# Step sizes' weight parts in one stationary operand, and the compression's first layer with gathered blocks stationary

## What is computed

```
u = rms_norm(h, norm_w)
z, xbc, dt = split(u @ in_w, ...)          # dt: 512 x 32
dt = softplus(dt + dt_bias)
```

```
blk = to_g(t)[:, :, cidx] + pe             # 2 groups x 31 blocks x 32 x 64
flat = blk.reshape(B, G, Nc, CMP_BLOCK * dh)
return gelu(flat @ w1) @ w2                # w1: 2048 x 128
```

## Time and profile before

| | |
|---|---|
| median of the runs | 1399.4 us |
| span of the profiled execution | 1396.6 us |
| instructions | 17863 |
| mean granted clock of TensorE | 0.996 |
| TensorE busy | 1355.5 us (97%) |
| VectorE busy | 831.2 us (60%) |
| ScalarE busy | 680.4 us (49%) |
| POOL busy | 529.8 us (38%) |

### The profile page before, as it was taken

The page is one execution under the profiler, slowest core; times in us unless marked ns, Lnnn a source line. Parts: engine busy times, 40 slices in busy tenths (PEclk is TensorE's granted clock), DMA queues, the critical chain, the costliest instruction groups (busy, mean ns, idle before and its releaser), DMA issues.

```text
span 1396.6 us, 17863 instructions
## 1 busy us (share of the span) xinstructions
PE 1355.5 (97%) x6632; PEld 1067.3 (76%) x6632; DVE 831.2 (60%) x1439; ACT 680.4 (49%) x1134; POOL 529.8 (38%) x259
## 2 busy tenths in 40 slices
PE   8999999999999999999999999999999999999997
PEld 6777777777778878757888887765667788888886
DVE  5576464657567754685677423478745654554666
ACT  6654635636366443685565312355545423232463
POOL 2553554635320034456100444136532655555300
PEclk9999999999999999999999999999999999999999
DMA  5222222222132223211233333130012333333331
GB/s 190 91 76 58 84 72 76 82 71 76 58 107 93 91 89 91 63 46 46 91 105 117 84 136 103 33 119 16 16 31 91 91 92 105 91 103 94 121 106 61
DMA packets 33221, 117.32 MB, mean 84 GB/s; under 512 B 3948, under 2 KB 4332, under 8 KB 32880
## 3 DMA queue, kind: packets, MB, share of 16 engines
q1 hardware_dynamic: 31976, 111.85, 26.0%
q10 hardware_dynamic: 1160, 4.34, 0.9%
HBM read 114.08 MB, written 2.10 MB: 83 GB/s over the span
## 4 chain that ended last, share of the span: by engine, by line
PE 88%; DVE 5%; ACT 3%; issue 2%; DMA 1%; POOL 1%; DVEq 0%; ACTq 0%
PE bank L1286 84%; PE bank L1740 1%; PE bank L1583 1%; ACT wsh L852 1%; POOL wsl L704 1%; DMA h<-in_xT 1%; DMA arena<-in_alibi 0%; POOL arena L762 0%; PE bank L1459 0%; DVE arena L1981 0%; PE bank L1494 0%; DVE arena L2273 0%; DVE arena L1901 0%; PE bank L1738 0%; DVE arena L2187 0%
## 5 line engine op out<-in xcount | busy, mean ns | idle before, releaser
L704 POOL TENSOR_TENSOR wsl<-ring,wsh 128x1024 fp32r<-128x1024 f32 x144 | 351.5, 2442 | 555.1 <-ACT wsh L852 554.9
L852 ACT ACTIVATE wsh<-ring 128x1024 fp32r<-128x1024 f32 x199 | 210.5, 1058 | 457.0 <-PE bank L1286 433.7
L1286 PE MATMUL bank<-parts1h,wsh 128*128 128x512 f32 (+1 forms) x736 | 292.2, 397 | 10.8 <-POOL wsl L704 3.5
L1286 PE MATMUL bank<-parts1h,wsl 128*128 128x512 f32 (+1 forms) x736 | 285.9, 388 | 0.0
L1286 PE MATMUL bank<-parts1l,wsh 128*128 128x512 f32 (+1 forms) x736 | 285.7, 388 | 0.0
L1286 PE MATMUL bank<-parts0h,wsh 128*128 128x512 f32 x704 | 281.2, 399 | 3.7 <-issue 1.3
L1286 PE MATMUL bank<-parts0h,wsl 128*128 128x512 f32 x704 | 274.5, 390 | 0.0
L1286 PE MATMUL bank<-parts0l,wsh 128*128 128x512 f32 x704 | 274.2, 390 | 0.0
L1286 PEld LDWEIGHTS bank<-parts1h,wsh 128*128 128x128 f32 x736 | 138.7, 188 | 47.4 <-issue 7.6
L1286 PEld LDWEIGHTS bank<-parts0h,wsh 128*128 128x128 f32 x704 | 132.2, 188 | 40.6 <-issue 9.1
L1286 PEld LDWEIGHTS bank<-parts1l,wsh 128*128 128x128 f32 x736 | 138.7, 188 | 28.9 <-issue 1.9
(11 more groups left out here) (318 smaller groups left out, 1796.8 us busy)
## 6 DMA issues: line engine op xcount, KB each, us to landing
ring<-in_wstream SPq DMA_DIRECT2D x206, 512.0 KB, 3.6
arena<-in_alibi ACTq DMA_DIRECT2D x2, 1024.0 KB, 6.0
outT<-arena SPq DMA_DIRECT2D x8, 256.0 KB, 3.1
h<-in_xT SPq DMA_DIRECT2D x2, 256.0 KB, 5.6
h<-in_xT ACTq DMA_DIRECT2D x2, 256.0 KB, 6.4
h<-in_xT SPq DMA_DIRECT2D x1, 512.0 KB, 8.4
h<-in_xT ACTq DMA_DIRECT2D x1, 512.0 KB, 9.3
arena<-in_frow ACTq DMA_DIRECT2D x1, 512.0 KB, 3.4
```

The lines of the kernel that those rows point to most:

```text
L704: return nc.gpsimd.tensor_tensor(dst, src, hi.bitcast(F32), ALU.subtract)
L852: nc.scalar.activation(wsh[n % NSET][:, :], src, ACT.Copy).then_inc(*done("high", ("high", L)))
L1286: return nc.tensor.matmul(*args, **kw)
```

## The change

For the step sizes the host lays the 32 weight columns down twice in each tile. ScalarE makes the high part of both copies, and POOL subtracts it in the second copy from the raw weights, in place, so that `wsh` holds high and low side by side and `wsl` isn't used. TensorE then needs two matmuls for each tile, one for each part of the activations, 16 in all; the result has 64 rows that are copied and transposed, and VectorE adds the two halves with one operation more.

In the first layer of the compression the operands change sides: 62 columns of `cblk` are stationary and 128 columns of weights are moving. The eight matmuls of a step write in turn to partitions 0 to 61 and 64 to 125 of the PSUM bank. The result is transposed against before and lies in two halves. A new step `cmpt j`, behind `mk 0` and behind `aq 0`, turns it: ScalarE copies both halves to SBUF (`ctok`), TensorE transposes that tile into a bank of the rotation, and VectorE in step `cmp j` copies one half and adds the other.

```diff
--- before.py
+++ after.py
@@ -218,10 +218,14 @@
             out.append(("mrcol",))
         if 1 <= i <= 2:
             out.append(("cmpq", 0, i - 1))
+        if i == 4:
+            out.append(("cmpt", 0))
         if i == 6:
             out.append(("cmp", 0))
         if 5 <= i <= 6:
             out.append(("cmpq", 1, i - 5))
+        if i == 8:
+            out.append(("cmpt", 1))
         if i == 9:
             out.append(("cmp", 1))
         if i == 11:
@@ -322,6 +326,8 @@
         if h + 1 == M_HEADS:
             return [("num", h)]
         return [("Mb", h + 1), ("num", h)] + [("KQ", h + 1, s) for s in range(NT)]
+    if k == "cmpt":
+        return [step]
     if k == "cmp2":
         return [("ckT",), ("cv",)]
     if k == "nS":
@@ -558,7 +564,7 @@
         zs = ar(16, GT, SEQ)
         xdt = [ar(20 + b, HPG, HD) for b in range(2)]
         xde = [ar(22 + b, HPG, HD) for b in range(2)]
-        dtf = ar(24, SEQ)[0:HEADS]
+        dtf = ar(24, SEQ)[0:2 * HEADS]
         rhead = [parts[1][0][:, 4 + 2 * b:6 + 2 * b, :].rearrange("p a (r i) -> p (a r) i", i=P) for b in range(2)]
         acT = parts[1][1][:, 4, :]
         lgrp = parts[1][1][:, 5, :]
@@ -636,6 +642,7 @@
 
         chid = ar(24, 2, 64)
         ctm = ar(24.25, 3, 64)
+        ctok = ar(25.625, P)
         vct = ar(24.75, 2, HD)[0:NC_BLK]
         scb = [ar(25 + b / 4, 4, NC_BLK) for b in range(2)]
         kcT = ar(25.5, NC_BLK)
@@ -711,8 +718,13 @@
                     src = ring[:, L % NSLOT, :]
                     if n is not None and not on_vector(step):
                         pool.wait_ge(*at("high", L))
-                        low(wsl[n % NSET][:, :], src, wsh[n % NSET][:, :])\
-                            .then_inc(*done("split", ("split", L), ("slot_free", L)))
+                        if b[0] == "dt":
+                            beside = wsh[n % NSET][:, :].rearrange("p (a b) -> p a b", a=KD)[:, :, HEADS:2 * HEADS]
+                            low(beside, src.rearrange("p (a b) -> p a b", a=KD)[:, :, HEADS:2 * HEADS], beside)\
+                                .then_inc(*done("split", ("split", L), ("slot_free", L)))
+                        else:
+                            low(wsl[n % NSET][:, :], src, wsh[n % NSET][:, :])\
+                                .then_inc(*done("split", ("split", L), ("slot_free", L)))
                 if k == "hn" and a[0] != "final":
                     for name in a[:1]:
                         hi, lo = (xgh, xgl) if name == "kv" else (hnh, hnl)
@@ -950,7 +962,7 @@
                             .then_inc(*done("zs", ("zs", g, i - 6), ("free", *step)))
                 if k == "dtl":
                     act.wait_ge(*at("raw_scaled", "dtl"))
-                    nc.scalar.activation(dtf, ps(step)[0:HEADS, :], ACT.Copy).then_inc(*done("dtf", ("dtf",), ("free", "dtl")))
+                    nc.scalar.activation(dtf, ps(step)[0:2 * HEADS, :], ACT.Copy).then_inc(*done("dtf", ("dtf",), ("free", "dtl")))
                 if k == "dt":
 
                     nc.scalar.activation(aneg[:, :], rowb[:, R_ALOG:R_ALOG + HEADS], ACT.Exp).then_inc(*done("aexp", ("aexp",)))
@@ -1146,6 +1158,15 @@
                 if k == "mo":
                     act.wait_ge(*at("scaled", *step))
                     nc.scalar.activation(moT[:, a[0], :], moT[:, a[0], :], ACT.Tanh, scale=0.5).then_inc(*done("mo", ("done", *step)))
+                if k == "cmpt":
+                    j = a[0]
+                    act.wait_ge(*at("mm", "chid", j))
+                    act.wait_ge(*at("cblk", 1))
+                    if j:
+                        act.wait_ge(*at("mm", "cmpt", 0))
+                    for o in (0, HD):
+                        last = nc.scalar.activation(ctok[o:o + 2 * NC_BLK, :], acc(("chid", j))[o:o + 2 * NC_BLK, 0:P], ACT.Copy)
+                    last.then_inc(*done("ctok", ("ctok", j), ("accfree", "chid", j)))
                 if k == "cmp":
 
                     act.wait_ge(*at("gelu_in", a[0]))
@@ -1303,6 +1324,12 @@
 
                 b = open_bank(job)
                 w = weights(name)
+                if name == ("dt",):
+                    for kt in range(KD):
+                        for part in range(2):
+                            last = mm(b[:, :], w[0][:, tok(kt)], src[part][:, kt, :], start=kt + part == 0, stop=kt + part == KD)
+                    last.then_inc(*used(name, ("mm", *job)))
+                    return
                 for kt in range(KD):
                     if normed == "raw":
                         pe.wait_ge(*at("raw", kt))
@@ -1426,7 +1453,7 @@
                     b = open_bank(("dt",))
                     pe.wait_ge(*at("dtf"))
                     for t in range(NT):
-                        last = nc.tensor.transpose(b[:, t * HEADS:(t + 1) * HEADS], dtf[:, tok(t)], ident[0:HEADS, 0:HEADS])
+                        last = nc.tensor.transpose(b[:, 2 * t * HEADS:2 * (t + 1) * HEADS], dtf[:, tok(t)], ident[0:2 * HEADS, 0:2 * HEADS])
                     last.then_inc(*done("mm", ("mm", "dt")))
                 if k == "cum":
                     b = open_bank(("cum",))
@@ -1624,9 +1651,14 @@
                     pe.wait_ge(*at("loaded", L))
                     w = ring[:, L % NSLOT, :]
                     for l in range(8):
-                        last = mm(b[:, 0:2 * NC_BLK], w[:, l * P:(l + 1) * P], cblk[j][:, 8 * q + l, :],
-                                  start=(q == 0 and l == 0), stop=(q == 1 and l == 7))
+                        o = HD * (l % 2)
+                        last = mm(b[o:o + 2 * NC_BLK, 0:P], cblk[j][:, 8 * q + l, :], w[:, l * P:(l + 1) * P],
+                                  start=(q == 0 and l < 2), stop=(q == 1 and l >= 6))
                     last.then_inc(*done("mm", ("slot_free", L), *([("mm", "chid", j)] if q == 1 else [])))
+                if k == "cmpt":
+                    b = open_bank(step)
+                    pe.wait_ge(*at("ctok", a[0]))
+                    nc.tensor.transpose(b[:, 0:P], ctok, ident).then_inc(*done("mm", ("mm", *step)))
                 if k == "cmp2":
                     b = open_bank(("ckT",))
                     pe.wait_ge(*at("gelu", 1))
@@ -1801,6 +1833,7 @@
                 for b, n in splits_at(step):
                     if n is not None and on_vector(step):
                         L = BLKNO[b]
+                        assert b[0] != "dt"
                         dve.wait_ge(*at("high", L))
                         low(wsl[n % NSET][:, :], ring[:, L % NSLOT, :], wsh[n % NSET][:, :])\
                             .then_inc(*done("split_dve", ("split", L), ("slot_free", L)))
@@ -1905,8 +1938,9 @@
                             x.then_inc(*done("conv", ("conv", g, i), ("free", *step)))
                 if k == "dt":
                     dve.wait_ge(*at("mm", "dt"))
-                    b = ps(("dt",))[:, 0:P].rearrange("p (a b) -> p a b", a=NT)
-                    link(nc.vector.tensor_tensor(dtmp, b, over(rowb[:, R_DTB:R_DTB + HEADS], NT, 1), ALU.add))
+                    b = ps(("dt",))[:, 0:2 * P].rearrange("p (a b) -> p a b", a=NT)
+                    link(nc.vector.tensor_tensor(dtmp, b[:, :, 0:HEADS], over(rowb[:, R_DTB:R_DTB + HEADS], NT, 1), ALU.add))
+                    link(nc.vector.tensor_tensor(dtmp, dtmp, b[:, :, HEADS:2 * HEADS], ALU.add))
                     nc.vector.scalar_tensor_tensor(dtmp2, dtmp, -1.0, dtmp, ALU.mult, ALU.min)\
                         .then_inc(*done("dtabs", ("dtabs",), ("free", "dt")))
                     dve.wait_ge(*at("dtln"))
@@ -2283,9 +2317,10 @@
 
                         dve.wait_ge(*at("cblk", 1))
                         link(nc.vector.memset(ctm[:, :, :], 0.0))
-                    dve.wait_ge(*at("mm", "chid", j))
-                    nc.vector.tensor_copy(x, acc(("chid", j))[:, 0:2 * NC_BLK].rearrange("p (g n) -> p g n", g=2))\
-                        .then_inc(*done("chidc", ("chidc", j), ("accfree", "chid", j)))
+                    dve.wait_ge(*at("mm", "cmpt", j))
+                    two = ps(("cmpt", j))[:, 0:P].rearrange("p (o n) -> p o n", o=2)[:, :, 0:2 * NC_BLK].rearrange("p o (g n) -> p o g n", g=2)
+                    link(nc.vector.tensor_copy(x, two[:, 0]))
+                    nc.vector.tensor_tensor(x, x, two[:, 1], ALU.add).then_inc(*done("chidc", ("chidc", j), ("free", "cmpt", j)))
                     dve.wait_ge(*at("chidc", j))
                     link(nc.vector.tensor_tensor(y, x, x, ALU.mult))
                     link(nc.vector.tensor_scalar(y, y, 0.044715, 1.0, ALU.mult, ALU.add))
@@ -2538,7 +2573,7 @@
             return w1[b[1]].reshape(CMP_BLOCK // 2, 2, HD, P)[8 * b[2]:8 * b[2] + 8].transpose(1, 2, 0, 3)
         if k == "dt":
 
-            w = np.concatenate([f["ssm_in_w"][0][:, -HEADS:], np.zeros((D, P - HEADS), np.float32)], 1)
+            w = np.concatenate([f["ssm_in_w"][0][:, -HEADS:]] * 2 + [np.zeros((D, P - 2 * HEADS), np.float32)], 1)
             return w.reshape(KD, P, P).transpose(1, 0, 2)
```

## The result

The change made the kernel slower by less than half a per cent. Its runs have a median of 1405.78 us against 1400.35 us for the kernel before beside it, a ratio of 1.0043 (95% interval 1.003 to 1.0057), some 6 us. Among the runs of the kernel before is a slow one of 1696.21 us, which lifts its medians a little and is left out of the ratios. Timed again later, beside other variants, the change had a ratio of 1.0053 (1.0037 to 1.0068), 7.4 us. The forecast was 1402.4, +3.0 us.

A forecast was written before the change was run, and what follows sets the result against it. TensorE, busy 97% of the span, was taken as the bound. Step sizes 0, groups -1.0 and `cmpt` +4.0 gave +3.0 us on the 1399.4 us median: 1402.4 us, range 1399.8 to 1406.5.

The forecast's parts named there:

- Step sizes, 0: At the start, 2.3 us saved on TensorE would be lost waiting for POOL's low half before `proj 0 9`: sum 0.
- Rival (b): The start's chain moves along with the shorter step sizes' product, so 2.3 us are won: 1400.1 us; chance 0.08.
- Groups: Four groups of compression matmuls, two pairs, each 0.5 us shorter; only each pair's first group counts: -1.0 us.
- the chain through the ring slot: First group's end frees a slot; DMA, ScalarE's conversion and POOL's low half follow before `mq 3`, 7.6 us in all.
- Rival (d): In the compression, the accumulating halves of the array don't overlap: 1403.6 us; chance 0.08.
- `cmpt`, 2.0 us each: Behind `mk 0` and `aq 0`, TensorE waits for ScalarE's copies, queued behind a weight conversion: 2 x 2.0 = 4.0 us.
- the row of 2.48 us: TensorE's old wait ending at 86.55; the clock stayed at 1.00 around it, cited against falls in new gaps.
- rival (a): TensorE's clock falls in the gap before `proj 0 9`, 1403.6 us; also in both `cmpt` gaps, 1407.0; chance 0.20.
- a drop of the clock near 36: Sign of a wrong forecast: TensorE's granted clock dropping near 36 us, behind the gap before `proj 0 9`, or near 822.

The follow-up runs named there:

- e1_step_sizes_alone: The step sizes' half of the change alone, the compression as in the kernel before: ratio 1.0005 (0.9994 to 1.0015) against the kernel before.
- e3_early_copies: The whole change with ScalarE's two copies made earlier, in the step of the pair's second group (`cmpq j 1`): ratio 0.9996 (0.9984 to 1.0009) against the kernel before.
- e8_change_again: The whole change unaltered, timed again beside other variants on one chip: ratio 1.0053 (1.0037 to 1.0068) against the kernel before, 7.4 us above it.
- e7_before_vector_low: The kernel before, with VectorE instead of POOL making the low parts for `proj 0 9` and `proj 0 0`: ratio 0.9985 (0.9974 to 0.9996) against the kernel before.

## Why the prediction was right in its steps and too low in its sum

**Step sizes, 0:** right. The gap was put at 3.0 us and is 3.2; `proj 0 0` stays in place against the row norm but for the clock, and the half by itself gives 1.0005. Rival (b) is out. One reading in it was wrong: POOL's low half of 256 columns was put at a quarter of 2.4 us and takes 1.28, which cost nothing, since it ends at 21.96 and TensorE comes at 22.10.

**Groups:** 0.5 us each was near: TensorE gains 0.6, since the step into the new form costs the 0.1 us that was put in. Of the pairs 1.0 us was expected and 1.5 measured. What was mis-sized is the start of the chain through the ring slot: it starts when the last matmul ends, and from the group's start that is 1.09 us now and was 1.89 before, a gain of 0.8 less the 0.1 (ScalarE's conversion comes 4.80 us behind the group's start, before it was 5.67). Rival (d) is out: halves that accumulate do overlap. The Trainium skill's rate of up to two, in "TensorEngine Tiling (Array Packing)", section Theoretical Speedup, agrees with 1.89 to 1.02 us, a factor of 1.85 between one half and two; against the old form, which the sum had to be made from, it is 1.7.

**`cmpt`, 2.0 us each:** right, 2.03 and 2.18. Moving the copies took both away.

**The clock:** here the forecast failed. The step said that new gaps bring no fall, by the row of 2.48 us whose clock stayed at 1.00, and gave rival (a) a chance of 0.20. Rival (a) is what happened, and with it came one of the prediction's own signs of being wrong, a drop of the clock near 36: a fall behind the gap before `proj 0 9`, priced there at +1.2, measured +0.9 (20.55 against 19.65 us from the row norm; +1.9 in the whole change again); and a fall behind one of the two waits, priced at 1.7, measured 1.70. The fault is in the evidence. That same wait of 2.48 us was followed by 0.51 in the trace after: one trace without a fall isn't proof that a gap of that length is safe. "TensorE: Matmul & The Clock Gate" in the Trainium skill, section Why this matters for your kernels, warns of gaps between bursts, and the traces agree, if not every time: in four profiles with the 3.2 us gap unfilled (after, `e1_step_sizes_alone`, `e3_early_copies`, `e8_change_again`) three have the fall and one hasn't. The falls at 87 and behind 1093 us in the profile after, which the profile of before lacks, are not put down to the change. The first stands in eight of the thirteen profiles, among them `e7_before_vector_low` and `e1_step_sizes_alone`, which have no new compression. The second stands in six of the ten profiles with the new compression and in none of the three without. Whether the change makes these more frequent stays open.

So of the measured 6.0 us 2.7 are steps, and the rest, as the profiles have it, falls that differ from run to run. The forecast time counted none of them; the range held the measured time because it reached over rival (a), and in part by luck, since the falls at old waits, which it priced nowhere, are in the profile too.

## What to carry to other kernels

Before a wait is put on a busy engine, look at what stands ahead of the awaited work in its engine's queue: here work for two steps later did, and moving two copies to a place where that engine idles turned a loss into a draw, and with the other half of the change undone into a gain of 2.5 us. Work taken off the bounding engine counts only where nothing else is due right behind it; a gap left open there can make later work slower, through the clock: in three of four profiles `proj 0 0` came 0.9 to 1.9 us later. And narrow stationary operands pay through column halves used side by side, not through the swap alone.

## What the runs showed of the hardware

- Behind the same wait in the same place the granted clock fell in some profiles and not in others: behind the 2.48 us at 84 us it was 1.00 in the profile before and 0.51 after, and eight of the thirteen profiles have a fall there. In the profile after a fall cost 1.65 us at 87 and 1.70 at 851.
- Sixteen fp32 instructions of 62 stationary and 128 moving columns took 1.02 us, from the first start to that of the next product, when outputs alternated between the partition halves, and 1.89 us when they didn't.
- POOL's subtraction of 256 columns in eight pieces of 32 took 1.28 us, as long as 512 in a row (1.28 to 1.30 us) and more than a quarter of the 2.39 us for 1024.
- Adding 3.1 us of matmuls to an idle gap kept the clock up and brought `proj 0 0` 0.95 us closer to `proj 0 9`.
